# Expert weights of a two-layer mixture-of-experts stage: each 2 MB slab sent as two transfers of 1 MB, with a wait and a release for each half

## What is computed

```
def expert_block(args):
    xb, e = args
    hb = jax.nn.silu(xb @ w_gate[e]) * (xb @ w_up[e])
    return hb @ w_down[e]
...
    y_rows = yb.reshape(n_rows, D)[dest]
    contrib = y_rows * gate.reshape(-1)[order][:, None].astype(y_rows.dtype)
    out = jnp.zeros((T, D), hf.dtype).at[tok].add(contrib)
```

## Time and profile before

| | |
|---|---|
| Time, median of 3 runs | 2198.55 us (2195.52 to 2200.14) |
| The profiled execution's own time | 2196.08 us |
| Its span, first to last instruction | 2194.3 us |
| Mean granted clock of TensorE | 0.918 |
| Busy: PE, PEld, DVE, ACT | 1820.2, 1177.4, 558.5, 330.6 us |
| Moved by DMA | 562.08 MB, 256 GB/s over the span |
| Expert slabs | 192 of 2048 KB (96 a layer) |

### The profile page before, as it was taken

The page is one execution under the profiler, slowest core; times in us unless marked ns, Lnnn a source line. Parts: engine busy times, 40 slices in busy tenths (PEclk is TensorE's granted clock), DMA queues, the critical chain, the costliest instruction groups (busy, mean ns, idle before and its releaser), DMA issues. The chain is left out here.

```text
span 2194.3 us, 21932 instructions
## 1 busy us (share of the span) xinstructions
PE 1820.2 (83%) x9506; PEld 1177.4 (54%) x9506; DVE 558.5 (25%) x1245; ACT 330.6 (15%) x685; POOL 0.2 (0%) x4
## 2 busy tenths in 40 slices
PE   7999866666667999976676666779999988989999
PEld 6788422212216878822222221668886875678844
DVE  4843200000003664310000000241422328410100
ACT  2241100000001233100000000211411115300000
POOL 0000000000000000000000000000000000000000
PEclk9999988888889999998878888889999989999999
DMA  7436899999997433699999999214341540134441
GB/s 327 185 116 255 333 428 428 428 427 428 428 428 306 158 131 139 234 420 427 428 427 428 428 427 428 119 61 130 132 152 64 171 154 1 39 115 154 153 153 58
DMA packets 40180, 562.08 MB, mean 256 GB/s; under 512 B 4464, under 2 KB 4464, under 8 KB 5744
## 3 DMA queue, kind: packets, MB, share of 16 engines
q1 hardware_dynamic: 40080, 560.62, 63.1%
HBM read 559.55 MB, written 1.05 MB: 255 GB/s over the span
## 5 line engine op out<-in xcount | busy, mean ns | idle before, releaser
L1171 PE MATMUL ps<-ring,hB 128*32 128x512 f32 x1344 | 195.9, 711 | 122.2 <-DMA ring<-in_stream 122.2
L1586 PE MATMUL ps<-hA,ring 128*128 128x256 f32 (+1 forms) x1280 | 280.8, 383 | 11.4 <-DVE hA L1931 11.4
L1586 PEld LDWEIGHTS ps<-hA,ring 128*128 128x128 f32 (+1 forms) x1280 | 240.4, 188 | 51.2 <-DVE hA L1931 12.2
L552 PE MATMUL ps<-hA,ring 128*128 128x256 f32 x1152 | 253.0, 380 | 0.0
L552 PEld LDWEIGHTS ps<-hA,ring 128*128 128x128 f32 x1152 | 217.7, 190 | 32.7 <-issue 3.7
L1171 PEld LDWEIGHTS ps<-ring,hB 128*32 128x32 f32 x1344 | 41.3, 120 | 274.1 <-DMA ring<-in_stream 138.2
L1171 PE MATMUL ps<-l_extra,hB 128*32 128x512 f32 x704 | 117.2, 800 | 77.0 <-DMA l_extra<-in_stream 77.0
L1182 PE MATMUL ps<-ring,l_work 128*32 128x512 f32 x704 | 105.8, 735 | 58.9 <-DMA ring<-in_stream 50.3
L1263 DVE TENSOR_TENSOR l_work<-ps,l_work 128x512 f32<-128x512 f32 x16 | 11.1, 692 | 435.2 <-ACT l_work L1237 435.2
L1171 PEld LDWEIGHTS ps<-l_extra,hB 128*32 128x32 f32 x704 | 23.1, 128 | 159.8 <-DMA l_extra<-in_stream 90.3
L945 DVE SCALAR_TENSOR_TENSOR l_extra<-l_extra,lpar 128x256 f32<-128x256 f32 x232 | 102.1, 481 | 3.6
(11 more groups left out here) (311 smaller groups left out, 1901.3 us busy)
## 6 DMA issues: line engine op xcount, KB each, us to landing
ring<-in_stream SPq DMA_DIRECT2D x189, 2048.0 KB, 37.7
l_extra<-in_stream SPq DMA_DIRECT2D x64, 2048.0 KB, 40.8
ring<-in_stream SPq DMA_DIRECT2D x6, 1792.0 KB, 16.5
ring<-in_stream SPq DMA_DIRECT2D x4, 1344.0 KB, 8.2
ring<-in_stream SPq DMA_DIRECT2D x2, 1764.0 KB, 9.5
ring<-in_bias SPq DMA_DIRECT2D x1, 3072.0 KB, 17.7
ring<-in_stream SPq DMA_DIRECT2D x2, 1024.0 KB, 29.8
xT<-in_xT SPq DMA_DIRECT2D x1, 1024.0 KB, 4.8
```

Of the source, the lines that this page charges most:

```text
L552: mm = self.nc.tensor.matmul(out[:, m * T:(m + 1) * T], w[:, k, c * P:(c + 1) * P], src[:, k, :], start=(k == 0), stop=(k == kc - 1))
L1171: mm = nc.tensor.matmul(out[js, :], x_slots[q % 2][:, c, js], w[:, 0, j * D + n0:j * D + n0 + FF], start=(c == 0), stop=(c == DC - 1))
L1586: mm = nc.tensor.matmul(out[0:width, m * T:(m + 1) * T], w[:, k, c * width:(c + 1) * width], src(k), start=(k == 0), stop=(k == kc - 1))
```

## The change

Each expert slab goes out as two transfers, columns 0 to 2047 and 2048 to 4095 of its rows (8 KB a row each). The first half counts on the slot's semaphore `landed`, the second on a new one, `landed_up`. In a slab the columns are laid out half by half: all four experts' gate columns in the first half and all up columns in the second (for down, the left 512 output columns of all four, then the right ones). PE waits for each half (`wait_half`) ahead of its four matmuls, in the same order of matmuls as before, and increments `half_used` (before: `slab_used`) after each half. SP waits before the first half for the first half of the slab that had the slot before, and before the second half for its second one; where one of the two isn't an expert slab, SP waits once, for all of it. ACT's copy of the left half of the result waits for the left half of the last slab only. The waits of the other steps keep their meaning, in half slabs. The overflow block reads the new layout.

```diff
@@ -200,6 +200,7 @@
 
 RING, EXTRA = 6, 3
 SLAB = 4096
+HALF = SLAB // 2
 
 
 class Slabs:
...
@@ -300,8 +304,9 @@
         put(chunked(np.asarray(a["w_conv_out"][l])))
         cols(np.asarray(a["w_out"][l]), 0, count=2)
         gu = np.stack([np.asarray(a["w_exp_gate"][l]), np.asarray(a["w_exp_up"][l])], axis=-2)
-        gu = gu.reshape(QUADS, QUAD, DC, P, 2 * FF).transpose(0, 2, 3, 1, 4)
-        dn = np.asarray(a["w_exp_down"][l]).reshape(QUADS, QUAD, FC, P, D).transpose(0, 2, 3, 1, 4)
+        gu = gu.reshape(QUADS, QUAD, DC, P, 2, FF).transpose(0, 2, 3, 4, 1, 5)
+        dn = np.asarray(a["w_exp_down"][l]).reshape(QUADS, QUAD, FC, P, 2, BANK).transpose(0, 2, 3, 4, 1, 5)
+        gu, dn = (x.reshape(QUADS, -1, P, SLAB) for x in (gu, dn))
         both = np.concatenate([gu, dn], axis=1).reshape(QUADS * QUAD_SLABS, P, SLAB)
         slabs.extend(both)
         put(chunked(np.asarray(a["w_ple_proj"][l])))
...
@@ -376,14 +382,31 @@
             i = self.issued
             rows, chunks, cols = self.slabs.shape[i]
             s, before = self.slabs.slot[i], self.slabs.before[i]
-            if before is not None and before >= self.known:
-                sp.wait_ge(*self.freed[before])
-            sp.dma_start(self.slot(s)[0:rows, 0:chunks * cols], self.stream[i, 0:rows, 0:chunks * cols]).then_inc(self.landed[s], 16)
+            halves = 2 if self.halved(i) else 1
+            n = chunks * cols // halves
+            for h in range(halves):
+                if before is not None and before >= self.known:
+                    if self.halved(before) and halves == 2:
+                        sem, value = self.freed[before]
+                        sp.wait_ge(sem, value - 1 + h)
+                    elif h == 0:
+                        sp.wait_ge(*self.freed[before])
+                sp.dma_start(self.slot(s)[0:rows, n * h:n * h + n], self.stream[i, 0:rows, n * h:n * h + n])\
+                    .then_inc((self.landed_up if h else self.landed)[s], 16)
             self.issued += 1
+
+    def halved(self, i):
+
+        return "moe" in self.slabs.name[i]
 
     def wait(self, pe, i):
         pe.wait_ge(self.landed[self.slabs.slot[i]], 16 * self.slabs.nth[i])
         return self.view(i)
+
+    def wait_half(self, pe, i, h):
+        s = self.slabs.slot[i]
+        pe.wait_ge((self.landed_up if h else self.landed)[s], 16 * (self.slabs.nth_half if h else self.slabs.nth)[i])
+        return self.slot(s)[:, h * HALF:(h + 1) * HALF]
 
     def free(self, i, sem, value):
 
...
@@ -1164,25 +1187,23 @@
 
         def gate_up(q, c):
             i = m0 + q * QUAD_SLABS + c
-            w = store.wait(pe, i)
-            for out, n0 in ((gate_bank, 0), (up_bank, FF)):
+            for h, out in enumerate((gate_bank, up_bank)):
+                w = store.wait_half(pe, i, h)
                 for j in range(QUAD):
                     js = slice(SLOTS * j, SLOTS * (j + 1))
-                    mm = nc.tensor.matmul(out[js, :], x_slots[q % 2][:, c, js], w[:, 0, j * D + n0:j * D + n0 + FF],
-                                          start=(c == 0), stop=(c == DC - 1))
-            mm.then_inc(self.slab_used, 1)
-            store.free(i, self.slab_used, i - m0 + 1)
+                    mm = nc.tensor.matmul(out[js, :], x_slots[q % 2][:, c, js], w[:, j * FF:(j + 1) * FF], start=(c == 0), stop=(c == DC - 1))
+                mm.then_inc(self.half_used, 1)
+            store.free(i, self.half_used, 2 * (i - m0 + 1))
 
         def down(q, f):
             i = m0 + q * QUAD_SLABS + DC + f
-            w = store.wait(pe, i)
-            for half in range(2):
+            for h in range(2):
+                w = store.wait_half(pe, i, h)
                 for j in range(QUAD):
                     js = slice(SLOTS * j, SLOTS * (j + 1))
-                    mm = nc.tensor.matmul(y_banks[half][js, :], hidT[:, f, js], w[:, 0, j * D + half * BANK:j * D + (half + 1) * BANK],
-                                          start=(f == 0), stop=(f == FC - 1))
-            mm.then_inc(self.slab_used, 1)
-            store.free(i, self.slab_used, i - m0 + 1)
+                    mm = nc.tensor.matmul(y_banks[h][js, :], hidT[:, f, js], w[:, j * BANK:(j + 1) * BANK], start=(f == 0), stop=(f == FC - 1))
+                mm.then_inc(self.half_used, 1)
+            store.free(i, self.half_used, 2 * (i - m0 + 1))
 
         pe.wait_ge(self.emptied["htok"], 4)
         gather(0)
...
@@ -1233,13 +1254,13 @@
 
         gathered(0)
         for q in range(QUADS):
-            act.wait_ge(self.slab_used, q * QUAD_SLABS + DC)
+            act.wait_ge(self.half_used, 2 * (q * QUAD_SLABS + DC))
             nc.scalar.activation(self.silu_slots, ps[0][:], ACT.Silu).then_inc(self.gu_silu, 1)
             if q < QUADS - 1:
                 gathered(q + 1)
             act.wait_ge(self.turned_hid, q + 1)
             nc.scalar.copy(flat(self.hidT), ps[5][:]).then_inc(self.hidT_ready, 1)
-            act.wait_ge(self.slab_used, (q + 1) * QUAD_SLABS)
+            act.wait_ge(self.half_used, 2 * (q + 1) * QUAD_SLABS - 1)
             if q:
                 act.wait_ge(self.part_filled, 4 * q)
             nc.scalar.copy(self.y_slots[:, 0:BANK], ps[2][:]).then_inc(self.y_left, 1)
...
@@ -1261,7 +1282,7 @@
                 add_parts(q - 1)
             dve.wait_ge(self.gu_silu, q + 1)
             vec.tensor_tensor(self.hid_slots, ps[1][:], self.silu_slots, ALU.mult).then_inc(self.hid_ready, 1)
-            dve.wait_ge(self.slab_used, (q + 1) * QUAD_SLABS)
+            dve.wait_ge(self.half_used, 2 * (q + 1) * QUAD_SLABS)
             vec.tensor_copy(self.y_slots[:, BANK:], ps[3][:]).then_inc(self.y_right, 1)
         add_parts(QUADS - 1)
```

More of the change, by code:

```diff
@@ L212, in __init__ @@
         self.first = {}
+        self.halves, self.nth_half = {s: 0 for s in range(RING + EXTRA)}, []
     def add(self, name, slots, rows, chunks, cols):
@@ L222, in add @@
         self.nth.append(self.count[s])
+        self.halves[s] += "moe" in name
+        self.nth_half.append(self.halves[s])
         self.shape.append((rows, chunks, cols))
@@ L360, in __init__ @@
         self.landed = [ctx.enter_context(nc.semaphore(f"landed{i}")) for i in range(RING + EXTRA)]
+        self.landed_up = [ctx.enter_context(nc.semaphore(f"landed_up{i}")) for i in range(RING + EXTRA)]
         self.freed = []
@@ L490, in __init__ @@
          self.pair_ready, self.pexp_ready, self.mask_ready, self.pick_ready, self.pick_gate_ready, self.zeroed, self.x_filled,
-         self.x_copied, self.put_filled, self.put_copied, self.slab_used, self.gu_silu, self.hid_ready, self.turned_hid,
+         self.x_copied, self.put_filled, self.put_copied, self.half_used, self.gu_silu, self.hid_ready, self.turned_hid,
          self.hidT_ready, self.y_left, self.y_right, self.part_filled, self.part_added, self.spread, self.renormed) = (sem(n) for n in (
@@ L495, in __init__ @@
              "pair_ready", "pexp_ready", "mask_ready", "pick_ready", "pick_gate_ready", "zeroed", "x_filled",
-             "x_copied", "put_filled", "put_copied", "slab_used", "gu_silu", "hid_ready", "turned_hid",
+             "x_copied", "put_filled", "put_copied", "half_used", "gu_silu", "hid_ready", "turned_hid",
              "hidT_ready", "y_left", "y_right", "part_filled", "part_added", "spread", "renormed"))
@@ L1338, in _ @@
                             sp.wait_ge(filled["down" if j == 2 else "gate_up"], q * (4 * QUAD) + (m * 4 + 4))
-                            one = slabs[bass.ds(q, 1), :, :, m * D:(m + 1) * D].rearrange("b j p n -> p (b j) n")
-                            w = one[:, DC:] if j == 2 else one[:, 0:DC, j * FF:(j + 1) * FF]
-                            sp.dma_start(weights(j), w).then_inc(self.over_landed[j], 16)
+                            for h in range(2) if j == 2 else (j,):
+                                w = slabs[bass.ds(q, 1), :, :, h * HALF + m * FF:h * HALF + (m + 1) * FF].rearrange("b j p n -> p (b j) n")
+                                if j == 2:
+                                    sp.dma_start(weights(j)[:, :, h * BANK:(h + 1) * BANK], w[:, DC:]).then_inc(self.over_landed[j], 16)
+                                else:
+                                    sp.dma_start(weights(j), w[:, 0:DC]).then_inc(self.over_landed[j], 16)
             @block.tensor
@@ L1362, in _ @@
                         mm.then_inc(filled["gate_up"], 1)
-                    pe.wait_ge(self.over_landed[2], (e + 1) * 16)
+                    pe.wait_ge(self.over_landed[2], (e + 1) * 32)
                     pe.wait_ge(emptied["gate_up"], e * 4 + 8)
```

## The result

| | before | after |
|---|---|---|
| Median, us | 2198.55 (2195.52 to 2200.14) | 2210.73 (2208.92 to 2211.35) |
| Ratio to before, 95% interval | | 1.0055 (1.0040 to 1.0069) |
| Profiled execution's own time, its span | 2196.08, 2194.3 | 2211.35, 2209.6 |
| Mean granted clock | 0.918 | 0.898 |

The medians are of five executions each. The change costs 12.2 us. Forecast were 9.6 us, 2208.2, with a range of 2200.5 to 2216.5.

The account below looks back on a forecast made before the run. The DMA weight stream was taken to bound the expert stages. Packets at +13.05 us less 3.4 us at the stages' ends gave +9.6 us on the median 2198.55, so 2208.2 us, range 2200.5 to 2216.5.

Parts of the forecast that it names:

- The bound and the place: Expert stages of both layers: DMAs full at 427 to 428 GB/s, so only plateaus and their ends can change.
- the stretches outside the plateaus unchanged within 1 us: Everything outside the two expert stages: a sign expected in the new profile, times the same within 1 us.
- The packet's price: Steady plateau: 8 KB packets cost 0.075 us more a slab, for 87 slabs in 2 layers +13.05 us.
- The view of packets: Packet durations on full DMA queues: two 8 KB packets against one of 16 KB, 0.09 to 0.10 us a slab.
- the two landings: Projection slab behind the last expert slab: a half lands in 2.48 us, two halves take 0.06 us more than one slab.
- The start: Start of each expert stage: half release lets SP reissue half a slab earlier, -0.86 us a layer.
- The end: End of each expert stage: 0.86 us of work behind the last landing in place of 1.72, -0.86 us a layer.
- Rival B: Stage ends: shorter PE bursts leave the clock at 1.2 GHz, 4.7 us a layer, +19 us, 2217.6; chance 0.08.
- Rival A: Plateaus: added packets cost only their small fixed part, +2.7 us, 2201.2, not visibly slower; chance 0.17.
- C: Whole expert stages: earlier buffer release makes the kernel faster, by over 4.4 us; chance 0.04.
- D: Halves aren't two transfers in effect, PE always finds both; without the ends' gain +13 us, 2211.6; no separate chance.
- An edit at nothing: Added waits, increments and SP issues (0.33 us each, 2.45 us available) in the stages: no cost expected.

Follow-up runs that it names:

- c2_last_half: The changed kernel, but PE waits for whole slabs except at each stage's last slab, taken half by half; 2209.65 us, ratio 1.0061 to the kernel before.
- b3_ends: Changed layout, but only each layer's first reissued and last slab go as halves, the others as one 16 KB-row transfer; 2196.21 us, 0.9997 of the kernel before.
- a3_whole_wait: The changed kernel, but PE waits for both halves before a slab's first matmul; 2211.51 us, ratio 1.0057 to the kernel before.
- b1_fill: The changed kernel plus one matmul with unused result ahead of each half's wait in each layer's last quad; 2207.78 us.
- c3_ends_fill: `b3_ends` plus the matmuls with unused results in each layer's last quad; 2188.41 us, ratio 0.9973 to the kernel before the change.
- d1_fill_early: `c3_ends_fill` with the same added matmuls one quad earlier, the seventh of eight; 2195.82 us, ratio 0.9991 to the kernel before the change.

## Why the prediction was right, and where it was off

**The bound and the place: right.** The stages have 11.25 of the 15.3 us between the two profiles, and they got longer as the DMA rate says. The sign "the stretches outside the plateaus unchanged within 1 us" failed, with -1.2, +3.6 and +1.6 us.

**The packet's price: right, at +13.05 us forecast.** Taken were 0.075 us a slab. By the rate it is 0.079, by the stages of one-transfer kernels 0.075 with 8 KB rows and 0.22 with 4 KB. The view of packets (0.09 to 0.10, called an upper value) was too high by a fifth to a third, and the two landings (0.06) too low by a fifth; that a value chosen between them came out so near is in part luck. The Trainium skill, DMA: Bandwidth & Descriptors, section "Why small descriptors are slow (HBM only)", has about three cycles a packet, by the page's 850 MHz an estimate of 0.0035 us. That is well under half of the 0.0091 to 0.0094 us that the two runs show here.

**The start: right.** SP's first reissue came 1.13 us behind PE's start in place of 1.98, 0.85 us earlier, against 0.86.

**The end: mis-sized, both by the gain that didn't come and by a loss.** The step said that 0.86 us of work stays behind the last landing in place of 1.72. The half wait did this where the clock was full (`c2_last_half` and `b3_ends`: 1.06 and 1.07 us for the last half). In the changed kernel the last half takes 1.93 us, and the combine 5.25 to 5.77 in place of 3.88. Per layer that is 0.87 + 1.4 to 1.9 us, 2.2 to 2.8, and over two layers about 5 us. From the start of the last half to DVE's copy are 2.0 us, where the prediction's sign was one or less from the landing on. The sum with what was measured is 13.05 - 1.7 for the starts, +0 for the last slabs, +1.4 and +1.8 for the combines of the profiled execution: +14.5, against 15.3 between the two profiles and 12.2 between the medians. The first two terms are 11.35 and the stages measured 11.25. Outside of the stages the sum has +3.1 and the profiles +4.05, of which -1.2 ahead of the first stage and some 2.2 ahead of the second have no term, so that the total fits better than its parts.

**The nearness of the number owes something to luck.** The median that the forecast was added to, 2198.55, is the highest of the five sets of the kernel before; the others, of 12 to 21 runs, are 2196.45 to 2197.95. Against those the changed kernel's two medians are 12.8 to 15.0 us slower, 3 to 5 us more than the forecast 9.6.

**Rival B** was the right mechanism for the ends with a chance far too low (0.08): four ends of four have it, and the prediction's own sign for it, bursts at 0.5 at the end, came true. Its argument against, that "the combine comes after the same idle time as now", looked at the idle time alone and not at the shorter bursts before it. Its price (4.7 us a layer) was too high, since the clock comes back inside the combine (0.74 on average over it). That half waits lower the clock is shown by the runs' mean (0.892 to 0.899 against 0.914 or more) and on the first plateau (0.78 against 0.83 to 0.88); that they cause the low clock at the ends is shown by odds only, as `a3_whole_wait` has it too.

**Rival A** falls with the plateau at 421 GB/s, **C** with the stages. **D** is answered at the ends: PE did find the halves one by one, 2.49 us apart.

**An edit at nothing that wasn't.** "SP issues an expert transfer in 0.33 us" held only for the first reissues. On the plateau most issues take 2.13 us (about one in seven some 6), and landings come after 27.0 us in place of 37.7, the medians of the two pages for `ring`:

```profile
405.86 2.13 SPq L394 DMA_DIRECT2D l_extra<-in_stream  x1
```
```profile
ring<-in_stream SPq DMA_DIRECT2D x258, 1024.0 KB, 27.0
```

5.4 slabs were on order in place of 7.7. It was harmless, since the DMA engines stayed busy throughout (101.1%), but not for the reason given.

## What to carry to other kernels

Where a stretch runs at the full rate of the DMAs, a finer split of transfers can help only where the queue is empty: at its start and at its end. Splitting each row in two has a price for each packet, paid by every slab (here 87 of 96 a layer), so split the first and the last transfer and leave the rest whole. In this kernel that gave about 2 us a stage, too little to show in the whole time. An end that is meant to get shorter must be costed at both clock levels, and the change's own effect on the clock just ahead of it belongs to the cost.

## What the runs showed of the hardware that was not expected

- A packet costs 0.0091 to 0.0094 us beyond its bytes in a full queue: 427, 421 and 409 GB/s with rows of 16, 8 and 4 KB.
- Two transfers of rows 0 to 63 and 64 to 127 into the partitions of the same numbers, in turn, run at 215 GB/s with all 16 engines busy; even and odd rows in turn run at 427.
- SP's issue of a transfer is held up when enough is on order (2.13 to 4.92 us in place of 0.33). Counted back from landing minus issue, at the end of an issue some 90 packets an engine were on order with two transfers in 8 KB rows ((27.0 - 2.13) / 2.49 = 10 transfers of 9), 95 with one (27.9 / 4.985 x 17), and 121 with 4 KB rows (18.8 / 5.13 x 33). No single limit of packets or of transfers fits all three; the rule stays open.
- With work that is thrown away in PE's gaps ahead of a barrier, PE's next work started 5.5 us earlier in one layer of each of two profiles (`b1_fill`, `c3_ends_fill`), and not in the other layer nor in `d1_fill_early`. Why is open.
- Taking weights in half-slab bursts at the same load lowered the mean granted clock of a run from 0.914 or more to 0.892 to 0.899.
